# Key projection of a mixture-of-experts and hybrid-mixer kernel as three products of rounded parts, with its casts and loads ahead of the values and the first modulation slot behind the queries

## The reference, cut to what matters

```python
p = h @ w_in + b_in                      # h: normalised and modulated x, or context
q_pre, k_pre, v, o = jnp.split(ml_p, 4, axis=-1)       # 512 columns each
qk = jax.nn.silu(short_conv(jnp.concatenate([q_pre, k_pre], axis=-1), conv_w, rows, row_len))
...
modulate(h, shift, scale) = h * (1.0 + scale[:, None, :]) + shift[:, None, :]
```

## Time and profile before

| | |
|---|---|
| median of three runs | 2381.88 us (2381.68 to 2383.93) |
| profiled execution | 2381.2 us, of which the span in the trace is 2379.4 us |
| PE busy | 2028.2 us, 85% of the span |
| POOL busy | 1003.3 us, 42% |
| VectorE, ACT busy | 777.1 us and 722.0 us |
| HBM read | 674.02 MB, 285 GB/s over the span |

### The profile page before, as it was taken

The page is one execution under the profiler, slowest core; times in us unless marked ns, Lnnn a source line. Parts: engine busy times, 40 slices in busy tenths (PEclk is TensorE's granted clock), DMA queues, the critical chain, the costliest instruction groups (busy, mean ns, idle before and its releaser), DMA issues.

```text
span 2379.4 us, 31423 instructions
## 1 busy us (share of the span) xinstructions
PE 2028.2 (85%) x13234; PEld 1410.6 (59%) x13234; DVE 777.1 (33%) x1490; ACT 722.0 (30%) x859; POOL 1003.3 (42%) x327
## 2 busy tenths in 40 slices
PE   9999997566666666666669999999999999999998
PEld 5888962111211112111128887888887887898887
DVE  4594842111111111111112445433313244534332
ACT  2356310000000000000004545544543454644452
POOL 1376520000000000000008765787887774887886
PEclk9999998878788888778789999999999999999999
DMA  9684599999999999999997544566656643666653
GB/s 358 190 291 130 188 400 428 427 427 429 428 429 428 428 430 428 428 429 428 429 417 264 168 159 120 172 198 209 197 189 221 214 160 106 185 179 195 212 189 129
DMA packets 245335, 680.19 MB, mean 286 GB/s; under 512 B 8215, under 2 KB 173192, under 8 KB 218731
## 3 DMA queue, kind: packets, MB, share of 16 engines
q1 hardware_dynamic: 241808, 672.41, 74.8%
q10 hardware_dynamic: 2603, 4.30, 0.7%
q0 software_dynamic: 816, 1.94, 0.2%
HBM read 674.02 MB, written 4.59 MB: 285 GB/s over the span
## 4 chain that ended last, share of the span: by engine, by line
PE 59%; DMA 35%; DVE 3%; ACT 1%; issue 1%; POOL 0%; SPq 0%; POOLq 0%; DVEq 0%; ACTq 0%
PE bank L2122 58%; DMA ring_sb<-w_exp 34%; PE bank L2125 2%; DMA ring_sb<-w_ada 1%; DVE bank L1291 1%; DVE x_sb L1291 1%; DVE arena_sb L1288 0%; DVE bank L1288 0%; DVE sm_sb L1868 0%; ACT ring_parts L1118 0%; DMA ring_sb<-w_in 0%; POOL ring_parts L830 0%; DMA ring_sb<-w_ffn_down 0%; POOLq L250 0%; POOL ring_parts L851 0%
## 5 line engine op out<-in xcount | busy, mean ns | idle before, releaser
L851 POOL TENSOR_TENSOR ring_parts<-ring_sb,ring_parts 128x2048 fp32r<-128x2048 f32 (+2 forms) x185 | 843.8, 4574 | 1200.7 <-ACT ring_parts L1118 1200.3
L2122 PE MATMUL bank<-arena_sb 128*32 128x512 f32 (+10 forms) x2862 | 373.2, 543 | 130.5 <-DMA arena_sb<-w_exp 121.0
L2122 PE MATMUL bank<-arena_parts,ring_parts 128*128 128x256 f32 (+1 forms) x2480 | 480.7, 329 | 0.9 <-DVE arena_parts L1288 0.9
L2122 PE MATMUL bank<-hT_parts,ring_parts 128*128 128x256 f32 (+1 forms) x2208 | 461.0, 325 | 3.3 <-ACT ring_parts L1118 2.3
L2122 PE MATMUL bank<-ring_sb,arena_sb 128*32 128x512 f32 (+1 forms) x2240 | 274.5, 633 | 190.7 <-DMA ring_sb<-w_exp 189.8
L1118 ACT CAST ring_parts<-ring_sb 128x2048 fp32r<-128x2048 f32 x186 | 351.2, 1888 | 213.4 <-DMA ring_sb<-w_in 96.3
L2122 PEld LDWEIGHTS bank<-arena_parts,ring_parts 128*128 128x128 f32 x2480 | 385.0, 190 | 45.0 <-DVE arena_parts L1288 1.1
L1288 DVE TENSOR_TENSOR arena_sb<-bank,arena_sb 128x512 f32<-128x512 f32 (+4 forms) x240 | 138.5, 600 | 768.0 <-PE bank L2122 670.7
L2122 PEld LDWEIGHTS bank<-hT_parts,ring_parts 128*128 128x128 f32 x2208 | 356.1, 190 | 39.8 <-ACT ring_parts L1118 3.0
L2122 PEld LDWEIGHTS bank<-arena_sb 128*32 128x32 f32 (+5 forms) x2862 | 151.7, 143 | 321.4 <-DMA arena_sb<-w_exp 169.2
L2122 PEld LDWEIGHTS bank<-ring_sb,arena_sb 128*32 128x32 f32 x2240 | 73.3, 128 | 379.7 <-DMA ring_sb<-w_exp 281.2
(11 more groups left out here) (287 smaller groups left out, 1302.4 us busy)
## 6 DMA issues: line engine op xcount, KB each, us to landing
ring_sb<-w_exp SPq DMA_DIRECT2D x96, 2048.0 KB, 36.0
arena_sb<-w_exp SPq DMA_DIRECT2D x93, 2048.0 KB, 36.1
ring_sb<-w_in SPq DMA_DIRECT2D x92, 1024.0 KB, 5.3
ring_sb<-w_ada SPq DMA_DIRECT2D x24, 1024.0 KB, 10.6
ring_sb<-w_ffn_gate SPq DMA_DIRECT2D x22, 1024.0 KB, 5.3
ring_sb<-w_ffn_up SPq DMA_DIRECT2D x22, 1024.0 KB, 5.3
ring_sb<-w_ffn_down SPq DMA_DIRECT2D x22, 1024.0 KB, 4.9
ring_sb<-w_in SPq DMA_DIRECT2D x42, 512.0 KB, 5.4
```

Source lines behind the costliest of these rows:

```text
L851: g.tensor_tensor(low, half(n)[0], high.bitcast(F32), ALU.subtract).then_inc(s["lo_ready"], 1)
L2122: return M.matmul(o, l, r, start=first, stop=last)
```

## The change

- The key columns come in two half-filled slots (`S_K`, 256 columns each, 1 MB), are split into parts, and both `kx` and `kc` become three products of rounded parts, 96 matmuls each in place of 32 plain ones. `kx` starts only when x is rounded (`x_high`) and not tile by tile.
- ACT rounds both key slots before it modulates its tiles of x, and both value slots earlier than before; POOL makes the key slots' low parts before the late loads. VectorE subtracts for x's low part before the context's statistics.
- The values of x come between `kx` and `kc`, with all products of the high weights before those of the low ones.
- `ada1.0` moves behind the queries, on PE and in the ring; it takes slot 10, and `ada1.3` takes slot 13 and is multiplied behind `xrow`. All slots from `hy0` on are numbered one higher.
- One spectrum moves from ahead of `adacol0` to behind it.

```diff
@@ plan_units
-    u.add("spec0", 5, "AV")
+    u.add("spec0", 4, "AV")
     u.add("ada0.1", 1)
-    u.add("spec5", 1)
+    u.add("spec4", 1)
     u.add("adacol0", 1)
     u.add("unused", 5)
-    u.add("spec6", 2, "AV")
+    u.add("spec5", 3, "AV")
     u.add("kx", 2, "A")
     u.add("hc", 4, "AV")
+    u.add("vx", 2)
     u.add("kc", 2, "A")
-    u.add("ada1.0", 1, "A")
-    u.add("vx", 2)
     u.add("vc", 2)
...
     u.add("q1", 1, "A")
+    u.add("ada1.0", 1, "A")
     u.add("ada1.1", 1)
     u.add("ada1.2", 1, "A")
-    u.add("ada1.3", 1)
     u.add("crow", 2)
     u.add("xrow", 2)
+    u.add("ada1.3", 1)
@@ slots
-        S_KC = len(slots)
-        slots.append((w_cols(w_in, ML0 + 512, 512), U.at("kc", 1)))
-        ada_slot(1, 0)
+        S_K = in_slots(ML0 + 512, ("kc", 0), ("kc", 1))
...
         S_Q = in_slots(ML0, ("q0", 0), ("q1", 0))
-        for i in range(1, 4):
+        for i in range(4):
             ada_slot(1, i)
@@ SyncE
-                if n == S_KC:
+                if n == S_K + 1:
                     sp.dma_start(ctxn, a["ctx"][0].rearrange("(t p) d -> p t d", p=P)).then_inc(s["ctx_landed"], 16)
@@ GpSimd
-            pool.wait_ge(s["unit_done"], U.at("spec5") + 1)
-            for dst, src in late_loads:
...
             in_mixer = split_slots.index(S_BR)
-            low_parts(0, in_mixer)
+            low_parts(0, 2)
+            pool.wait_ge(s["unit_done"], U.at("spec4") + 1)
+            for dst, src in late_loads:
+                g.dma_start(dst, src).then_inc(s["late_landed"], 16)
+            g.memset(vx[:, :, :, 128:129], 1.0)
+            g.memset(vc[:, :, :, 128:129], 1.0).then_inc(s["vaug_ones"], 1)
+            low_parts(2, in_mixer)
@@ ScalarE
-            for i in (0, 2, 4):
-                spectrum("spec0", i, i)
...
+            spectrum("spec0", 0, 0)
+            spectrum("spec0", 2, 2)
+            high_part(S_K)
+            high_part(S_K + 1)
...
-            spectrum("spec6", 0, 6)
             act.wait_ge(s["x_mod_act"], KD - BY_DVE)
             act.wait_ge(s["x_mod_dve"], BY_DVE)
             A.copy(hx_pair[0], modulated).then_inc(s["x_high"], 1)
-            act.wait_ge(s["unit_done"], U.at("spec6", 1) + 1)
+            spectrum("spec5", 0, 5)
+            spectrum("spec5", 2, 7)
...
+            high_part(S_V)
             act.wait_ge(s["ctx_var"], 1)
             A.activation(sm[:, 10:12], sm[:, 6:8], ACT.Sqrt).then_inc(s["ctx_sqrt"], 1)
+            high_part(S_V + 1)
...
-            high_part(S_V)
-            high_part(S_V + 1)
             raw("kc", 2, 16, 2)
-            ada_row(1, 0)
@@ VectorE
-            spectrum("spec6", 1, 7)
...
+            dve.wait_ge(s["x_high"], 1)
+            tt(hx_pair[1], modulated, hx_pair[0].bitcast(F32), ALU.subtract).then_inc(s["x_split"], 1)
             dve.wait_ge(s["ctx_landed"], 16)
             mean_square(ctxn, 2, 2)
...
-
-            dve.wait_ge(s["x_high"], 1)
-            tt(hx_pair[1], modulated, hx_pair[0].bitcast(F32), ALU.subtract).then_inc(s["x_split"], 1)
+            spectrum("spec5", 1, 6)
...
             conv(0, kT[:, 0:2], D_MLC + 4, 8, 4, U.at("kx", 0))
+            dve.wait_ge(s["c_high"], 1)
+            tt(hc_pair[1], modulated, hc_pair[0].bitcast(F32), ALU.subtract).then_inc(s["c_split"], 1)
...
             ada_row(1, 1)
-            ada_row(1, 3)
...
             give(V.tensor_copy(rw(3), take("xrow", 1)[0:4, :]))
+            ada_row(1, 3)
@@ TensorE
+            def key_products(j, kx):
+
+                c = slice(j * P, (j + 1) * P)
+                o = [b[:, j * T:(j + 1) * T] for b in kx]
+                for i in range(2):
+                    if j == 0:
+                        pe.wait_ge(s["pre_hi"], split_slots.index(S_K + i) + 1)
+                    for q in range(KD):
+                        mm(o[i], part(S_K + i, 1)[:, q, c], hx_pair[0][:, q], q == 0, False)
+                pe.wait_ge(s["x_split"], 1)
+                for i in range(2):
+                    for q in range(KD):
+                        mm(o[i], part(S_K + i, 1)[:, q, c], hx_pair[1][:, q], False, False)
+                for i in range(2):
+                    if j == 0:
+                        pe.wait_ge(s["pre_lo"], split_slots.index(S_K + i) + 1)
+                    for q in range(KD):
+                        ins = mm(o[i], part(S_K + i, 0)[:, q, c], hx_pair[0][:, q], False, q == KD - 1)
+                    if j == 1:
+                        close(ins)
+
+            pe.wait_ge(s["x_high"], 1)
             kx = [open_unit("kx", i) for i in range(2)]
...
+            for j in range(2):
+                key_products(j, kx)
             pe.wait_ge(s["ctx_norm"], 1)
             turn("hc", ctxn)
-            gemm_slot_T(S_KC, "kc", 0, modulated, "hc")
-            ada_product(1, 0)
-            for name, pair, made in (("vx", hx_pair, "x_split"), ("vc", hc_pair, "c_split")):
-                pe.wait_ge(s[made], 1)
...
+            def values(name, pair):
+
+                banks = [open_unit(name, t) for t in range(2)]
+                c = [slice(t * P, (t + 1) * P) for t in range(2)]
+                for t in range(2):
+                    for q in range(KD):
+                        if t == 0 and q % 4 == 0:
+                            pe.wait_ge(s["pre_hi"], split_slots.index(S_V + q // 4) + 1)
+                        w = part(S_V + q // 4, 1)[:, q % 4]
+                        mm(banks[t][:], pair[0][:, q, c[t]], w, q == 0, False)
+                        mm(banks[t][:], pair[1][:, q, c[t]], w, False, False)
+                for t in range(2):
+                    for q in range(KD):
+                        if t == 0 and q % 4 == 0:
+                            pe.wait_ge(s["pre_lo"], split_slots.index(S_V + q // 4) + 1)
+                        ins = mm(banks[t][:], pair[0][:, q, c[t]], part(S_V + q // 4, 0)[:, q % 4], False, q == KD - 1)
+                    close(ins)
+
+            values("vx", hx_pair)
+            pe.wait_ge(s["c_split"], 1)
+            slots_T(S_K, "kc", hc_pair)
+            values("vc", hc_pair)
...
-            for i in range(1, 4):
+            for i in range(3):
                 ada_product(1, i)
...
+            ada_product(1, 3)
             slots_T(S_HY[0], "hy0", hx_pair)
```

57 lines of the change are left out of this document (8 added, 49 removed).

## The result

The changed kernel takes 2389.83 us (median of 9) beside 2382.82 us of the kernel before (median of 9, measured with it): a ratio of 1.0032, 95% interval 1.0022 to 1.0041. The forecast was 2386.5 with a range up to 2389.5: 4.6 us more than before, where the medians give 7.0. The direction of every step was right and one of the four was far too small.

A forecast was written before the change was run, and what follows sets the result against it. PE was taken to bound the mixer, so a microsecond there moves the end by one. Terms -4.6 + 5.2 + 1.5 + 2.5 = +4.6, added to the median 2381.88, gave 2386.5 us; range 2380.0 to 2389.5.

The forecast's parts named there:

- Step 1: At `kx` and `kc`: 96 products take 11.7 us each; with a 0.18 us wait gone, -4.6 us in all.
- Step 2: At the start of `kx`: VectorE's five operations, slowed beside POOL, take 6.8 us; `kx` starts at 49.9, +5.2 us.
- first rival: Ahead of `kx`: VectorE keeps its pace beside POOL, `kx` starts at 45.8; 2381.7 us, chance 0.18.
- Step 3: Within `kx`: waiting for x's low part and a slow clock after idling together cost +1.5 us; `kx` ends at 63.2.
- Step 4: At `hy0`: its load lands 4.3 us later, PE arrives 1.8 us later, so the stall grows by +2.5 us.
- own range: For the whole kernel: the forecast's narrower range, 2384.5 to 2388.5 us, chance 0.52.
- The rivals: VectorE keeps pace at `kx` (0.18), load queue keeps up at `hy0` (0.10), clock stays low (0.12), neither wait exists (0.08).
- The slower one: At `kx`: PE's clock stays at 1.2 GHz for 6.4 us after the restart, +1.7 us; 2388.2 us, chance 0.12.

The follow-up runs named there:

- e11_lows_last: e10_ada_back, with GpSimd waiting for VectorE's five modulating operations and `kx` making its products with GpSimd's low parts last; 2380.59 us, ratio 0.9992.
- e1_pool_waits: The changed kernel, with GpSimd waiting for VectorE's five modulating operations before making the key matrices' low parts; ratio 1.0032.
- e12_fill_hy: The changed kernel, with 16 overwritten identity products filling TensorE's wait for GpSimd's low parts at `hy0`; 2387.01 us, ratio 1.0022.
- e3_ada_moved: The kernel before, with only the slot moves: `ada1.0` behind the queries, `ada1.3` behind the gate rows; old key products; 2388.38 us, ratio 1.0028.
- e10_ada_back: The changed kernel, with `ada1.0` back ahead of the queries (behind the context's values) and `ada1.3` ahead of the gate rows; 2382.36 us, ratio 1.0000.
- e2_hy_first: The changed kernel, with `hy0`'s two half slots ahead of `ada1.3` in the ring, and that slot's product and row addition behind `hy0`; 2400.64 us, ratio 1.0074.
- e9_row_ahead: e2_hy_first, with VectorE adding the row of `ada1.3` before the two convolutions of `hy0`; 2390.79 us, ratio 1.0040.

## Why the prediction was wrong

- **What bounds the kernel, and that a shift in the mixer reaches the end:** right. The shift is 7.98 us at 147 us and 7.97 at 297, and the profiled times lie 9.2 apart.
- **Step 1, the products:** right. `kx` without waits is 96 products in 11.5 us (e11_lows_last, 45.47 to 56.99; forecast 11.7), and `kc` takes 11.47.
- **Step 2, the start of `kx`:** right in mechanism and close in size: 48.93 against the forecast 49.9 (which is 5.1 us after 44.76, and not the 5.2 of the sum), the five operations 6.30 us against 6.8, and e1_pool_waits shows the cause by taking it away. The rule of the Trainium skill on which the first rival hung (SBUF — State Buffer, "Who interferes with whom": an operation of the tensor_scalar kind can take the port pair that it shares with GpSimd) is borne out by this case's traces: 6.30 us beside POOL and 1.70 without it. The first rival falls.
- **Step 3, behind the start:** right within 1 us. Forecast +1.5; from 48.93 to 63.06 `kx` takes 14.1 us where 11.7 was its work, +2.4. It ends at 63.06 (forecast 63.2), and that this is so close is luck: a start 1.0 us too late in the forecast and a slow clock 0.9 us too cheap cancel. The gate products start 0.5 us earlier than before, where the same sum had them 0.3 later.
- **Step 4, `hy0`: this step failed.** It said +2.5 us. From the start of the gate products to the turning of the columns it is 40.40 us before and 48.85 after; less the 1.92 us of `ada1.0`'s own products, that is **+6.5**. Three terms were too small. The slow clock behind the wait was missing altogether: 11.88 - 9.86 = 2.0 us, which e12_fill_hy takes off. I had used this very rule at `kx` and did not apply it to the wait of 3.5 us that my own sum put here. The landing came 0.9 us later than worked out (127.0 instead of 126.6, on a scale that itself had moved 0.5 earlier). And POOL's four subtractions took 6.36 us instead of 5.04, beside VectorE's scans and subtractions of those microseconds. Together, less the 0.3 us by which PE came later to `hy0` than the sum had it, these two make the waits 5.36 us instead of 3.5. The mechanism, order of PE's work and 2 MB more in the queue, is borne out by e3_ada_moved, e10_ada_back and the start of `hy0` in e2_hy_first.
- **The sum:** step 4 gives 4.0 us too little, steps 1 to 3 some 0.7 too much, and 4.6 + 4.0 - 0.7 = 7.9 is what the milestones show. The medians, measured side by side, lie 7.0 us apart: that is inside the range's +7.6, outside the +6.6 of the forecast's own range, and the time came out 0.3 us above 2389.5 in part because the kernel before, too, stood 0.9 us higher than the median that the sum was added to. The range held the loss of a long slow spell at one place; two places have one.
- **The rivals:** none of the four came. The slower one (2388.2) was nearest, and its spell is what `kx` got: 6.8 us at the slow clock, of which 5.8 lay on products. It was priced at 6.4 us, where the earlier trace rows give 6.8 for the stretch from 389 to 396 (0.64 + 6 + 0.2).

What stays open: how POOL's 6.36 us come about was not tried alone, and what holds e9_row_ahead was read from its trace and not tested.

## What to carry to other kernels

Price every wait of TensorE twice: the wait, and the slow clock that may lie behind it. At `kx` and `hy0` it lay behind every unfilled wait of 2.95 us or more, and cost 2.0 us where it was measured alone. A slot that moves back in a ring of loads can cost more than its own products (here 6.4 us, with the products the same in both places), since what stands behind it is issued later and queued behind more bytes. When two edits each remove one of two waits in series, each alone may measure as nothing; test them together before dropping either.
